# A gated stage's first projection cut into 512-row by 512-column half units, with its first 128 tokens evacuated ahead and one lower half made on GpSimd

## The reference, cut to what matters

```
x = x + rms_norm(ffn(h), ffn_post_norm)          # end of the ffn stage
hn = rmsnorm(x, norm_mix_g)                      # start of the gated stage
z = gelu(hn @ w_in)          # w_in 1024 x 4096; u = first 2048 columns, v = last 2048
u, v = split(z, 2)
v = layernorm(v, ln_g, ln_b)                     # over 2048 columns, for each token
sv = einsum('gij,bnjgc->bnigc', ws, vb) + b_s    # per block of 128 tokens, 8 groups
x = x + (u * sv) @ w_out                         # w_out 2048 x 1024
```

## Time and profile before

| | |
|---|---|
| median of 3 runs | 991.94 us (989.93 to 992.95) |
| the profiled execution | 990.83 us, its span 989.0 us |
| TensorE (PE) busy | 968.7 us, 98% of the span |
| VectorE (DVE) / ScalarE (ACT) / GpSimd (POOL) busy | 641.3 / 500.6 / 35.1 us |
| gated stage's v units on PE | from 378.23 to 428.26 us |
| granted clock, mean | 0.997 |

### The profile page before, as it was taken

The page is one execution under the profiler, slowest core; times in us unless marked ns, Lnnn a source line. Parts: engine busy times, 40 slices in busy tenths (PEclk is TensorE's granted clock), DMA queues, the critical chain, the costliest instruction groups (busy, mean ns, idle before and its releaser), DMA issues.

```text
span 989.0 us, 16482 instructions
## 1 busy us (share of the span) xinstructions
PE 968.7 (98%) x6739; PEld 901.2 (91%) x6739; DVE 641.3 (65%) x803; ACT 500.6 (51%) x666; POOL 35.1 (4%) x46
## 2 busy tenths in 40 slices
PE   7999999999999999999999999999999999999996
PEld 7999998899999998999999999999899899999995
DVE  5666757687777777587668654555767665454553
ACT  5765464565454556444336434434656464434432
POOL 1000001200000000000001000001000000000000
PEclk9999999999999999999999999999999999999998
DMA  9933213466565545555455565655464446565641
GB/s 280 246 114 122 85 44 96 148 226 213 170 205 177 183 158 155 186 170 171 171 170 184 183 200 177 205 170 186 124 159 171 128 145 218 178 203 176 206 129 42
DMA packets 128590, 165.04 MB, mean 167 GB/s; under 512 B 20862, under 2 KB 111419, under 8 KB 128411
## 3 DMA queue, kind: packets, MB, share of 16 engines
q1 hardware_dynamic: 127067, 159.57, 50.1%
q0 software_dynamic: 1312, 4.68, 1.6%
q10 hardware_dynamic: 160, 0.07, 0.0%
HBM read 163.26 MB, written 1.05 MB: 166 GB/s over the span
## 4 chain that ended last, share of the span: by engine, by line
PE 90%; DVE 4%; ACT 2%; DMA 2%; issue 1%; POOL 0%; POOLq 0%; SPq 0%; DVEq 0%; ACTq 0%
PE ps L240 27%; PE ps L241 27%; PE ps L242 27%; PE ps L1798 2%; PE ps L1177 1%; DMA raw<-in_w_in_dram 1%; DVE w_lo L218 1%; PE ps L1198 1%; ACT w_hi L204 1%; PE ps L1064 1%; PE ps L1793 1%; DVE union L2221 1%; PE ps L451 1%; PE ps L1187 0%; DMA X<-in_x_dram 0%
## 5 line engine op out<-in xcount | busy, mean ns | idle before, releaser
L218 DVE TENSOR_TENSOR w_lo<-raw,w_hi 128x2048 fp32r<-128x2048 f32 (+2 forms) x149 | 338.9, 2276 | 164.2 <-ACT w_hi L204 164.2
L204 ACT ACTIVATE w_hi<-raw 128x2048 fp32r<-128x2048 f32 (+2 forms) x149 | 283.3, 1902 | 137.6 <-PE ps L242 130.4
L240 PE MATMUL ps<-hT_hi,w_hi 128*128 128x256 f32 x1192 | 339.7, 285 | 2.0 <-DVE hT_lo L412 1.6
L241 PE MATMUL ps<-hT_hi,w_lo 128*128 128x256 f32 x1192 | 337.2, 283 | 0.0
L242 PE MATMUL ps<-hT_lo,w_hi 128*128 128x256 f32 x1192 | 337.2, 283 | 0.0
L240 PEld LDWEIGHTS ps<-hT_hi,w_hi 128*128 128x128 f32 x1192 | 228.4, 192 | 4.6 <-issue 1.3
L241 PEld LDWEIGHTS ps<-hT_hi,w_lo 128*128 128x128 f32 x1192 | 228.5, 192 | 1.7
L242 PEld LDWEIGHTS ps<-hT_lo,w_hi 128*128 128x128 f32 x1192 | 228.4, 192 | 0.0
L240 PE MATMUL ps<-w_hi,act_hi 128*128 128x512 f32 x416 | 163.3, 392 | 0.0
L241 PE MATMUL ps<-w_hi,act_lo 128*128 128x512 f32 x416 | 162.4, 390 | 0.0
L242 PE MATMUL ps<-w_lo,act_hi 128*128 128x512 f32 x416 | 162.0, 389 | 0.0
(11 more groups left out here) (298 smaller groups left out, 899.6 us busy)
## 6 DMA issues: line engine op xcount, KB each, us to landing
raw<-in_mlp_w_dram SPq DMA_DIRECT2D x64, 1024.0 KB, 5.3
raw<-in_w_up_dram SPq DMA_DIRECT2D x22, 1024.0 KB, 5.1
raw<-in_a_w_in_dram SPq DMA_DIRECT2D x16, 1024.0 KB, 5.3
raw<-in_w_in_dram SPq DMA_DIRECT2D x12, 1024.0 KB, 6.6
raw<-in_w_down_dram SPq DMA_DIRECT2D x11, 1024.0 KB, 4.9
raw<-in_a_w_out_dram SPq DMA_DIRECT2D x8, 1024.0 KB, 4.8
raw<-in_w_out_dram SPq DMA_DIRECT2D x4, 1024.0 KB, 5.0
raw<-in_b_w_o_dram SPq DMA_DIRECT2D x4, 1024.0 KB, 5.0
```

Of the source, the lines that this page charges most:

```text
L204: nc.scalar.activation(w_hi[:, s, 0:n], raw[:, r, 0:n], ACT.Copy).then_inc(hi_ready, 1)
L218: nc.vector.tensor_tensor(w_lo[:, s, 0:n], raw[:, r, 0:n], w_hi[:, s, 0:n].bitcast(F32), ALU.subtract).then_inc(lo_ready, 1)
L240: nc.tensor.matmul(o, a[0], b[0], start=start, stop=False, skip_group_check=shared)
L241: nc.tensor.matmul(o, a[1], b[0], start=False, stop=False, skip_group_check=shared)
```

## The change

- A v unit is now 512 rows of K (half h) by 512 columns (quarter q): two units make a quarter of v. TensorE makes 4 x 3 matmuls of 512 columns for each token block from each unit, into a whole PSUM bank for each block. The Gelu takes 512 columns at a time, the partial statistics too.
- The eight 128x256 evacuations of hT become sixteen 128x128 ones, each with its own counter, in the order h0 tb0, h0 tb1, h1 tb0, h1 tb1. TensorE starts its products on tb 0; the transposes of tb 1 and of the second half come between its products. `turns_by_block`, and the 12 matmuls in it, is no longer called for this stage.
- VectorE's order at the hand-over is written anew: lower halves of tb 0 stand ahead of the closing of pieces 2 and 3.
- The lower half of unit u0+1 is made by GpSimd, right behind its second inverse root, and no longer by VectorE.

The diff, cut to its core:

```diff
+        def half_cols(w, c0, h):
+            src = w[h * D // 2:(h + 1) * D // 2, c0:c0 + 512].rearrange("(k p) n -> p k n", p=P)
+            return (UNIT, lambda slot: (raw[:, slot, 0:UNIT].rearrange("p (k n) -> p k n", n=512), src))
...
-                for j in range(8):
-                    unit(cols(a_in, GATE + j * UC))
+                for q in range(4):
+                    for h in range(2):
+                        unit(half_cols(a_in, GATE + q * 512, h))
...
+        BLOCKS = [(t, tb) for h in range(2) for tb in range(TB) for t in range(4 * h, 4 * h + 4)]
+        def block_at(i):
+            return (W[1], W[2], W[3], ACC[0], ACC[1])[i % 5][:, i // 5 * P:(i // 5 + 1) * P]
+        def block_turn(pe, n, h, tb):
+            pe.wait_ge(x_done, 4 * (n - 1) + 2 * tb + h + 1)
+            for i in range(8 * h + 4 * tb, 8 * h + 4 * tb + 4):
+                t, tb = BLOCKS[i]
+                if i > 4:
+                    pe.wait_ge(b_lo, i - 4)
+                pe.transpose(block_at(i), X[:, tb, t * P:(t + 1) * P], ident[:]).then_inc(b_tr, 1)
+        def block_hi(act, gain):
+            for i, (t, tb) in enumerate(BLOCKS):
+                act.wait_ge(b_tr, i + 1)
+                nc.scalar.mul(hT_hi[:, t, tb * P:(tb + 1) * P], block_at(i), par[:, gain + t:gain + t + 1]).then_inc(b_hi, 1)
+        def block_lo(dve, gain, i0, i1):
+            for i in range(i0, i1):
+                t, tb = BLOCKS[i]
+                dve.wait_ge(b_hi, i + 1)
+                nc.vector.scalar_tensor_tensor(hT_lo[:, t, tb * P:(tb + 1) * P], block_at(i), par[:, gain + t:gain + t + 1],
+                                               hT_hi[:, t, tb * P:(tb + 1) * P].bitcast(F32), ALU.mult, ALU.subtract).then_inc(b_lo, 1)
+        def split_lo_pool(pool, u):
+            n, s, r = units[u][0], u % SPL, u % RAW
+            pool.wait_ge(hi_ready, u + 1)
+            pool.wait_ge(lo_ready, u)
+            nc.gpsimd.tensor_tensor(w_lo[:, s, 0:n], raw[:, r, 0:n], w_hi[:, s, 0:n].bitcast(F32), ALU.subtract).then_inc(lo_ready, 1)
...
 (post_dve)
             mean_square(0)
             close(0)
             close(1)
-            times_rows(2)
-            mean_square(1)
-            times_rows(3)
-            close(2)
-            close(3)
-            norm_lo(dve, n, gain)
+            if by_block:
+                block_lo(dve, gain, 0, 1)
+                mean_square(1)
+                block_lo(dve, gain, 1, 4)
+                times_rows(2)
+                close(2)
+                times_rows(3)
+                block_lo(dve, gain, 4, 8)
+                close(3)
+                block_lo(dve, gain, 8, 16)
...
+        V_BANKS = ((W[0], ACC[3]), (W[1], W[2]), (W[0], W[3]), (W[1], W[2]))
+        def gmlp_pe(pe, n, f):
+            def v_part(q, h, tb):
+                u = u0 + 2 * q + h
+                if tb == 0:
+                    pe.wait_ge(lo_ready, u + 1)
+                w = weights(u, 4)
+                for k in range(4):
+                    if q == 0:
+                        if k == 2 and tb == 0 and h == 0:
+                            block_turn(pe, n, 0, 1)
+                        if k == 2 and tb == 1 and h == 0:
+                            block_turn(pe, n, 1, 1)
+                        pe.wait_ge(b_lo, 8 * h + 4 * tb + k + 1)
+                    mm = mm3(V_BANKS[q][tb][:], [x[:, 4 * h + k, tb * P:(tb + 1) * P] for x in HT], [x[:, k, :] for x in w],
+                             h == k == 0, h == 1 and k == 3)
+                if tb:
+                    mm.then_inc(unit_used, 1)
+                elif h:
+                    mm.then_inc(s_v, 1)
+            block_turn(pe, n, 0, 0)
+            for q in range(4):
+                if q > 1:
+                    pe.wait_ge(s_g, 2 * q - 3 if q == 2 else 4)
+                for h in range(2):
+                    for tb in range(TB):
+                        if q == h == 0 and tb:
+                            block_turn(pe, n, 1, 0)
+                            pe.wait_ge(r_t, 8)
+                        v_part(q, h, tb)
+                if q == 0:
+                    gmlp_ws_pe(pe, n)
+                elif q == 2:
+                    gmlp_rows_pe(pe)
...
-            pe.wait_ge(s_g, 7)
+            pe.wait_ge(s_g, 8)
...
 (gmlp_act, for each q: upper half of u0+2q+3, Gelu of tb 0, Gelu of tb 1, upper half of u0+2q+4)
+                    nc.scalar.activation(gv[:, tb, q * 512:(q + 1) * 512], V_BANKS[q][tb][:], ACT.Gelu,
+                                         scale=stat[:, 6 + tb:7 + tb]).then_inc(s_g, 1)
...
 (gpsimd, behind post_pool of the ffn stage)
+                if "gmlp" in stages[n + 1:n + 2]:
+                    split_lo_pool(pool, first_unit["gmlp"] + 1)
...
 (vector, after the hand-over)
-                    split_lo(dve, first_unit[st] + 1)
+                    if st != "gmlp":
+                        split_lo(dve, first_unit[st] + 1)
                     if n in AFTER_POST:
                         sums_dve(dve, n)
+                    if st == "gmlp":
+                        dve.wait_ge(lo_ready, first_unit[st] + 2)
                     split_lo(dve, first_unit[st] + 2)
...
 (tensor)
-                elif n in AFTER_POST:
+                elif n in AFTER_POST and st != "gmlp":
                     turns_by_block(pe, n)
```

More of the change, by code:

```diff
@@ L542, in post_dve @@
             close(1)
-            times_rows(2)
-            mean_square(1)
-            times_rows(3)
-            close(2)
-            close(3)
-            norm_lo(dve, n, gain)
+            if by_block:
[8 more added lines that the diff above has]
+                block_lo(dve, gain, 8, 16)
+            else:
+                times_rows(2)
+                mean_square(1)
+                times_rows(3)
+                close(2)
+                close(3)
+                norm_lo(dve, n, gain)
         def rows_load(pool, k, v):
@@ L966, in build @@
         lnp = cut(2 * GT)
-        bnst = cut(TB, GG, 6)
+        bnst = cut(TB, 4, 6)
         mv = cut(TB, 2)
@@ L1069, in gmlp_act @@
             u0 = first_unit["gmlp"]
-            for j in range(8):
-                if j == 0:
-                    act.wait_ge(n_rstd, TB * n + TB)
-                act.wait_ge(unit_used, u0 + j + 1)
-                for tb in range(TB):
-                    gelu = nc.scalar.activation(gv[:, tb, j * UC:(j + 1) * UC], W[j % 4][:, tb * UC:(tb + 1) * UC], ACT.Gelu,
-                                                scale=stat[:, 6 + tb:7 + tb])
-                gelu.then_inc(s_g, 1)
-                split_hi(act, u0 + j + 3)
-                if j == 5:
+            act.wait_ge(n_rstd, TB * n + TB)
+            for q in range(4):
+                split_hi(act, u0 + 2 * q + 3)
+                if q == 3:
                     act.wait_ge(row_ps, 2)
                     nc.scalar.copy(rrow, ACC[0][:, 0:S]).then_inc(row_sb, 1)
+                for tb in range(TB):
+                    if tb == 0:
+                        act.wait_ge(s_v, q + 1)
+                    else:
+                        act.wait_ge(unit_used, u0 + 2 * q + 2)
+                    nc.scalar.activation(gv[:, tb, q * 512:(q + 1) * 512], V_BANKS[q][tb][:], ACT.Gelu,
+                                         scale=stat[:, 6 + tb:7 + tb]).then_inc(s_g, 1)
+                split_hi(act, u0 + 2 * q + 4)
             plain_act(act, f, 3, ACT.Gelu, n)
@@ L1085, in gmlp_dve @@
             u0 = first_unit["gmlp"]
-            for j in range(8):
-                dve.wait_ge(s_g, j + 1)
+            for q in range(4):
+                split_lo(dve, u0 + 2 * q + 3)
                 for tb in range(TB):
-                    nc.vector.bn_stats(bnst[:, tb, j, :], gv[:, tb, j * UC:(j + 1) * UC]).then_inc(s_bn, 1)
-                if j == 7:
-                    dve.wait_ge(s_bn, 16)
+                    dve.wait_ge(s_g, 2 * q + tb + 1)
+                    nc.vector.bn_stats(bnst[:, tb, q, :], gv[:, tb, q * 512:(q + 1) * 512]).then_inc(s_bn, 1)
+                if q == 3:
+                    dve.wait_ge(s_bn, 8)
                     for tb in range(TB):
                         nc.vector.bn_aggr(mv[:, tb, :], bnst[:, tb, :, :].rearrange("p a b -> p (a b)")).then_inc(s_mv, 1)
-                split_lo(dve, u0 + j + 3)
-                if j == 2:
+                split_lo(dve, u0 + 2 * q + 4)
+                if q == 0:
                     gmlp_ws_dve(dve, n)
-                elif j == 5:
+                elif q == 2:
                     gmlp_rows_dve(dve)
@@ L2410, in build @@
         for st in stages:
-            n_hi_count.append(n_hi_count[-1] + 8)
-        n_tr_count = [sum(8 if m in UNSCALED else 4 for m in range(n)) for n in range(len(stages))]
+            n_hi_count.append(n_hi_count[-1] + (0 if st == "gmlp" else 8))
+        n_tr_count = [sum((8 if m in UNSCALED else 4) for m in range(n) if stages[m] != "gmlp") for n in range(len(stages))]
         last_unit = {st: (first_unit[stages[k + 1]] if k + 1 < len(stages) else NU) - 1 for k, st in enumerate(stages)}
```

(9 more changed lines are left out.)

25 lines of the change are left out of this document (4 added, 21 removed).

## The result

The changed kernel takes 993.55 us, the median of 12 runs (991.74 to 996.52), against 991.31 us for the kernel before (12 runs, 989.75 to 992.95): ratio 1.0025, 95% interval 1.0014 to 1.0035. Forecast were +2.8 us and 994.7; of the 1.15 us between 994.7 and 993.55, 0.63 is the kernel before, whose median was 991.94 when the forecast was made and 991.31 beside the changed kernel.

What follows compares the result with a forecast made beforehand. TensorE, busy 98% of the span, was taken as the bound. Hold +2.5 and width -2.0 gave +0.5; clock +2.3 made +2.8, a median of 994.7 us, 8-in-10 range 990.0 to 996.6.

Steps and rivals of the forecast that it cites:

- Width: Last six of eight v units: 512-column matmuls take 32.7 us instead of 34.7, 2.0 us less.
- The early start: Hand-over: TensorE starts its first v product at 376.3, 1.9 us before the 378.23 of the kernel before.
- The hold: Hand-over: GpSimd's 4.12 us subtraction holds VectorE's closing of piece 2 until 381.75; u0+1 ends 2.5 us later.
- Rival 2: Hand-over: closing not held, piece 2 closes at 378.5 and the clock stays up: -2.7 us, 989.2; chance 0.15.
- Rival 3: Hand-over: everything on VectorE held, blocks and gains from PSUM too: +1.5 on top, 996.3; chance 0.10 with a longer slow stretch.
- Rival 1: Hand-over: closing held, but the clock stays up: +0.5 us, 992.4; chance 0.20.
- my lower bound: GpSimd's operation in the earlier trace: own work only 3.46 us if held by VectorE's subtraction; piece 2 closes at 381.1.
- The clock: Hand-over: TensorE's clock falls to 1.2 GHz around its 4.1 us pause, costing +2.3 us (1.5 to 3.0).
- What was set at nothing: After the hand-over: u0+2's halves, VectorE's new wait, SP's queue and the last Gelu cost nothing; u0+2 cover 0.3 us.
- the second pause: Hand-over: TensorE's longest pause, after its first six products, from 377.7 to 381.8, 4.1 us.

Runs made afterwards that it cites:

- e4: Changed kernel's 512-column products alone, with the old hand-over, 12 idle matmuls and VectorE making u0+1's lower half: 989.48 us, ratio 0.9982 to the kernel before.
- e9: Changed kernel with piece 2's product with the gains written back to PSUM, so its closing reads one SBUF operand: 989.16 us, ratio 0.9985 to the kernel before.
- e2: Changed kernel with 15 idle matmuls on TensorE between its first six products and the transposes of tb 1: 992.28 us, ratio 1.0018 to the kernel before.
- e5: Kernel before with only u0+1's lower half moved from VectorE to GpSimd: 996.87 us, ratio 1.0060.
- e3: Changed kernel with GpSimd's subtraction cut into 8 instructions of 256 columns: 988.90 us, ratio 0.9985 to the kernel before.
- e1: Changed kernel with GpSimd subtracting only 8 of 2048 columns, output not the reference's: 988.78 us, ratio 0.9980 to the kernel before.
- e10: e7 with piece 2's product with the gains left in PSUM: 986.54 us, ratio 0.9954 to the kernel before.
- e6: Changed kernel with u0+1's lower half given back to VectorE, behind the sixteen blocks: 991.02 us, ratio 0.9999 to the kernel before.
- e7: Changed kernel with GpSimd's subtraction in 8 pieces and ScalarE's upper half of weights ahead of the squares of pieces 2 and 3: 987.80 us, ratio 0.9968 to before.

## Why the prediction was right, and which term was off

**Width.** -2.0 us forecast for six units; the part behind u0+1 went from 37.95 (390.31 to 428.26) to 36.11 us (392.87 to 428.98): -1.84. e4 gives the same 1.84, and so does every other kernel here with the wide products. The pace from the mixer's rows carried over.

**The early start.** First product forecast at 376.3, L + 3.7; measured L + 3.70. Blocks on ScalarE and VectorE take 0.26 a step (four in 1.13 and 1.12), I took 0.28 and 0.26.

**The hold.** Forecast for the end of piece 2's closing: 381.75, L + 9.12; measured 380.41, L + 9.29. GpSimd needed 4.52 us, not 4.12, within the 0.5 that I had allowed; the Trainium skill's 4.497 ("GPSIMD Engine Reference", "Elementwise — side-by-side cycle accounting") was the better price here. It started at L + 4.22 instead of L + 4.42, which took back half of that. Rival 2 (not held) is ruled out by the 4.19: GpSimd began 0.88 us ahead of the closing. Rival 3 (blocks and products from PSUM held too) is ruled out by the product at 375.44, 0.68, and by e9's four blocks. Rival 1 (the clock stays) is ruled out by the stretches above. The one row of before on which I put the whole term, a single 4.10, was typical: in after, e2 and e9 (its second closing) a closing ends 0.5 to 0.6 us behind GpSimd, and in e5 the two together 1.20 behind, one closing more. The length of GpSimd's own row, 4.12, was in part luck. It belongs to another operation, a product of raw and par, and began 0.66 us before VectorE's subtraction ended. e3 shows that GpSimd is held by such an instruction too, so its own work there was more like the 3.46 us of my lower bound (an estimate), and a hold made it look nearly as long as the subtraction is.

**The clock.** Right in kind, too large in size, and this is the mis-sized term: +2.3 forecast, **1.4** measured in the profiled execution. Unit u0+1 ended 12.46 us after the closing, against the 11.1 that I had summed up at full clock; e1, e3 and e10, whose clock stays at 1.00 over the hand-over, need 11.09, 11.08 and 11.09, so the sum was right and the 1.4 is the clock. The rows under it: the four transposes and the next products took about twice their pace until 383.5, 3.0 us of TensorE's work at half speed, so 1.5 lost. I had read the length of the slow stretch off the program's start, bounds 2.9 to 6.1 us, and taken the middle; here it was at the lower end. But 1.4 is not a constant either: in e5 and e6 the slow stretch lasts 6.8 us, which is above my upper bound of 6.1. The mean clocks of after's 12 runs lie between 0.992 and 0.996, those of before beside the experiments between 0.995 and 0.999, and the slowest run of after (996.52) has the lowest clock; 3.4 us at half clock is 0.0017 of such a mean. So some executions of after spent longer at the low clock than the profiled one (0.996), but whether at the hand-over or elsewhere, as e7 did near 145 us, is not shown. With 1.4 in place of 2.3 the forecast sum is +1.9; the closing came 0.17 us later than forecast and the width gave 0.16 less, which makes the +2.23 of the stretch. So +2.8 came near because 0.9 too much for the clock stood against 0.33 too little for the rest.

**What was set at nothing** stayed at nothing. The wanted upper and lower half of u0+2 came at about 393.6, TensorE's first product behind the spatial transposes is at 394.01, as the transposes let it: a cover of 0.4 where I had 0.3. No later quarter has a pause.

**What I missed.** That the pause before the first product can bring the clock down by itself (e2, e6). I had put the fall into the second pause alone; in after's profiled execution it was there, in others it need not have been. I had also overlooked that a fall can come with no change of mine near it (e2 and e7, near 145 us).

Not settled: how often each of the two pauses brings the clock down, since only one execution of each kernel is profiled, why e5's slow stretch lasted 6.8 us and after's 3.4 with nearly the same pause (4.31 and 4.01), and what brought the clock down near 145 us in e2 and e7. No kernel here varied the pause alone.

## What to carry to other kernels

Before moving an elementwise operation to GpSimd to relieve VectorE, look at which VectorE instruction issues next and what it reads: with two operands in SBUF it was held in every case here until the GpSimd instruction, which reads two operands in SBUF itself, was done. So the price is what is left of that one instruction, on whatever path VectorE is on, and GpSimd pays the same way when VectorE is first. Give the VectorE instruction one operand in PSUM, or cut GpSimd's work in pieces as short as the delay that can be borne. And on a kernel bound by TensorE, add to every new pause of a few us the price of a fall of the clock behind it (here 1.4 us or more), and treat idle matmuls that an edit takes out as a part of the edit, though no run here prices them.

## What the runs showed that I had not expected

- A near tie is enough: in e5 GpSimd was first by 0.05 us (375.44 against 375.49) and VectorE lost 4.23.
- Eight pieces of 256 columns take 6.57 us against 4.52 for one instruction, but only 5.6 of it is their own: 0.15 us for each instruction more. The rest is two pieces held by VectorE's closings (e3). In e10, where one closing has an operand in PSUM, the eight take 6.04, with one piece held.
- The clock fell 3.7 us behind the last product in after, about 2.7 behind TensorE's last work in the earlier trace rows, and in e2 and e6 in or right after a first pause of 1.7 us, with only four transposes between it and the pause before. In e7 and e2 it fell at 144.5 and 145.5, when TensorE had been busy for ten us since a pause of 0.52 us. So the length of the last pause did not tell whether it falls.
